# Tail of the expert stage: down 14 and its add-back ahead of gate-up 15, the last weight unit in column halves

## The reference, cut to what matters

```python
top_logit, top_idx = lax.top_k(logits, TOP_K)          # 4 of 32 experts, 256 tokens
top_w = jax.nn.softmax(top_logit, axis=-1)
gu = xb @ w_gate_up[e] + b_gate_up[e]                  # 1024 -> 2048
gate, up = jnp.split(gu, 2, axis=-1)
gate = jnp.minimum(gate, SWIGLU_LIMIT)
up = jnp.clip(up, -SWIGLU_LIMIT, SWIGLU_LIMIT)
act = (up + 1.0) * gate * jax.nn.sigmoid(SWIGLU_ALPHA * gate)
out = act @ w_down[e] + b_down[e]                      # 1024 -> 1024
y = sum over a token's 4 experts of top_w * out        # h = h + y
```

## Time and profile before

| what | us |
|---|---|
| median of 3 runs | 1254.1 |
| lowest, highest | 1253.24, 1254.36 |
| the profiled execution, its own time | 1252.16 |
| its span, first to last instruction | 1250.4 |
| TensorE busy in it | 1172.7 (94%) |
| VectorE, ScalarE busy | 302.8 (24%), 133.3 (11%) |
| transferred | 446.37 MB, mean 357 GB/s |

### The profile page before, as it was taken

The page is one execution under the profiler, slowest core; times in us unless marked ns, Lnnn a source line. Parts: engine busy times, 40 slices in busy tenths (PEclk is TensorE's granted clock), DMA queues, the critical chain, the costliest instruction groups (busy, mean ns, idle before and its releaser), DMA issues.

```text
span 1250.4 us, 14148 instructions
## 1 busy us (share of the span) xinstructions
PE 1172.7 (94%) x5825; PEld 651.9 (52%) x5825; DVE 302.8 (24%) x551; ACT 133.3 (11%) x270; POOL 6.5 (1%) x14
## 2 busy tenths in 40 slices
PE   9999999999999999989898989898898989898988
PEld 7877888888633445525353434343443424353533
DVE  2154222311302321303030303222121303030322
ACT  2233311101200010100000000001010100000001
POOL 0000001000000000000000000000000000000000
PEclk9999999999999999999999999999999999999999
DMA  9722322336799999999999999999999999999996
GB/s 379 323 99 97 119 102 101 135 135 268 279 420 427 418 428 428 428 427 428 429 428 429 430 428 428 429 429 428 428 429 428 428 429 429 428 428 430 428 420 276
DMA packets 38514, 446.37 MB, mean 357 GB/s; under 512 B 4016, under 2 KB 5168, under 8 KB 6352
## 3 DMA queue, kind: packets, MB, share of 16 engines
q1 hardware_dynamic: 37856, 443.63, 84.8%
q10 hardware_dynamic: 624, 2.25, 0.5%
HBM read 444.81 MB, written 1.05 MB: 357 GB/s over the span
## 4 chain that ended last, share of the span: by engine, by line
PE 68%; DMA 28%; issue 1%; DVE 1%; SPq 0%; ACT 0%; DVEq 0%
DMA ring<-in_w_down 21%; PE ps L512 20%; PE ps L808 16%; PE ps L831 11%; PE ps L797 4%; PE ps L771 4%; DMA arena<-in_w_down 4%; DMA ring<-in_w_gate_up 3%; PE ps L862 2%; PE ps L880 2%; PE ps L817 1%; DVE arena L1439 1%; PE ps L852 1%; PE ps L826 0%; PE ps L571 0%
## 5 line engine op out<-in xcount | busy, mean ns | idle before, releaser
L808 PE MATMUL ps<-ring,arena 128*64 128x512 f32 x1344 | 403.9, 612 | 37.3 <-DMA ring<-in_w_gate_up 32.2
L808 PEld LDWEIGHTS ps<-ring,arena 128*64 128x64 f32 x1344 | 132.6, 141 | 292.2 <-issue 292.2
L512 PE MATMUL ps<-arena,ring 128*128 128x256 f32 (+1 forms) x1184 | 268.1, 383 | 1.1 <-DVE arena L1320 1.1
L512 PEld LDWEIGHTS ps<-arena,ring 128*128 128x128 f32 x1184 | 221.0, 189 | 38.9 <-issue 6.6
L831 PE MATMUL ps<-ring,arena 128*64 128x512 f32 x672 | 200.7, 599 | 28.8 <-DMA arena<-in_w_down 19.9
L808 PE MATMUL ps<-arena 128*64 128x512 f32 x448 | 198.3, 595 | 0.0
L831 PEld LDWEIGHTS ps<-ring,arena 128*64 128x64 f32 x672 | 65.3, 138 | 148.2 <-issue 148.2
L1419 DVE COPY arena<-ps 128x1024 f32<-128x1024 f32 x16 | 19.6, 1225 | 418.8 <-PE ps L808 409.6
L831 PE MATMUL ps<-arena 128*64 128x512 f32 x224 | 101.8, 608 | 0.0
L1412 DVE TENSOR_TENSOR arena<-ps,arena 128x512 f32<-128x512 f32 x64 | 41.1, 684 | 147.4 <-PE ps L817 147.4
L1140 ACT ACTIVATE arena<-ps 128x1024 f32<-128x1024 f32 x16 | 16.4, 1024 | 557.1 <-PE ps L808 541.3
(11 more groups left out here) (210 smaller groups left out, 585.5 us busy)
## 6 DMA issues: line engine op xcount, KB each, us to landing
ring<-in_w_gate_up SPq DMA_DIRECT2D x95, 2048.0 KB, 26.9
ring<-in_w_down SPq DMA_DIRECT2D x47, 2048.0 KB, 24.2
arena<-in_w_gate_up SPq DMA_DIRECT2D x32, 2048.0 KB, 31.2
ring<-in_mix_w SPq DMA_DIRECT2D x37, 1024.0 KB, 5.4
arena<-in_w_down SPq DMA_DIRECT2D x16, 2048.0 KB, 26.1
ring<-in_w_down SPq DMA_DIRECT2D x2, 1024.0 KB, 29.0
arena<-in_consts ACTq DMA_DIRECT2D x1, 1424.0 KB, 12.4
arena<-in_xT SPq DMA_DIRECT2D x2, 544.0 KB, 4.3
```

The costliest lines, as they stand in the source:

```text
L512: last = mm(ps[:, PROJ + half, 0:rhs.shape[-1]], w[:, k, half * P:(half + 1) * P], rhs, start=(k == 0), stop=(k == KC - 1))
L808: last = mm(ps[half, bank + b], columns[:, j, half], w[x][:, at:at + 512], start=(j == 0), stop=(j == 7))
```

## The change

TensorE and SyncE get an order of their own for the end. The last 16 units are now 4 of down 14, 8 of gate-up 15 and 4 of down 15. TensorE does down 14 and add-back 14 and only then gate-up 15, hidden 15, down 15 and add-back 15. Of the gate-up units the first four are loaded as before (one expert's rows, used in twos) and the last four hold both experts' rows and are used one by one. Between the transposes of hidden 15 and down 15 stand 14 extra matmuls whose result nobody reads. The last unit of down 15 is loaded in four transfers, by column halves and experts; TensorE computes its left columns, the first group of the add-back, then its right columns and the other groups. VectorE and ScalarE follow in the same order: `weigh` and `add_up` of 14 and `weigh` of 15 ahead of `hidden` of 15, and the copy of the turned weights ahead of the sigmoid. The loop over the earlier pairs stays as it is.

```diff
--- before.py
+++ after.py
@@ -438,24 +438,31 @@
                     src = gate_up_source(lap, q) if q < 8 else down_source(lap_before, q - 8)
                     sp.dma_start(dst, src).then_inc(arrived, 16)
 
-            def last_gate_up_units(m):
+            def last_units(m):
+
+                for n in range(4):
+                    sp.wait_ge(gu_used, 8 * m + n + 5)
+                    dst, arrived, _ = place(m, n, 0)
+                    sp.dma_start(dst.rearrange("p (o n) -> p o n", o=2), down_both_source(14, n // 2, n % 2)).then_inc(arrived, 16)
                 for q in range(8):
-                    dst, arrived, _ = place(m, q, 0)
-                    slot_free(m, q)
-                    sp.dma_start(dst, gate_up_source(15, q)).then_inc(arrived, 16)
-
-            def last_down_units(m, odd, lap, first_q, pieces):
+                    sp.wait_ge(dn_used, 4 * m + q - 3)
+                    dst, arrived, _ = place(m, 4 + q, 0)
+                    if q < 4:
+                        sp.dma_start(dst, gate_up_source(15, q)).then_inc(arrived, 16)
+                    else:
+                        sp.dma_start(dst.rearrange("p (o n) -> p o n", o=2), both_experts_source(15, q)).then_inc(arrived, 16)
                 for n in range(4):
-                    dst, arrived, _ = place(m, first_q + n, odd)
-                    slot_free(m, first_q + n)
-                    src = down_both_source(lap, n // 2, n % 2)
-                    dst = dst.rearrange("p (o n) -> p o n", o=2)
-                    if n == 3 and pieces == 2:
-                        for jj in range(2):
-                            part = slice(jj * D, (jj + 1) * D)
-                            sp.dma_start(dst[:, :, part], src[:, :, part]).then_inc(tail_landed[jj], 16)
+                    sp.wait_ge(gu_used, 8 * m + 9 + n)
+                    dst, arrived, _ = place(m + 1, n, 1)
+                    if n < 3:
+                        sp.dma_start(dst.rearrange("p (o n) -> p o n", o=2), down_both_source(15, n // 2, n % 2)).then_inc(arrived, 16)
                     else:
-                        sp.dma_start(dst, src).then_inc(arrived, 16)
+                        dst = dst.rearrange("p (o j n) -> p o j n", o=2, j=2)
+                        src = w_down[30:32].rearrange("o (g p i j) n -> p g i o j n", g=2, i=2, j=2)[:, 1, 1]
+                        for c in range(2):
+                            part = slice(c * 512, (c + 1) * 512)
+                            for x in range(2):
+                                sp.dma_start(dst[:, x, :, part], src[:, x, :, part]).then_inc(tail_landed[c], 16)
 
             first_units()
             second_units()
@@ -469,9 +476,7 @@
                 lap_2 = sp.compute_val((m + 2) & 15)
                 pair_units(m, 0, lap_1, lap_0)
                 pair_units(m + 1, 1, lap_2, lap_1)
-            last_gate_up_units(last_m)
-            last_down_units(last_m, 0, 14, 8, 1)
-            last_down_units(last_m + 1, 1, 15, 0, 2)
+            last_units(last_m)
             for b in range(4):
                 sp.wait_ge(added, 4 * last_m + 5 + b)
                 sp.dma_start(out[:, 2 * b:2 * b + 2], x_sb[:, 2 * b:2 * b + 2, META:ALL]).then_inc(stored, 16)
@@ -842,9 +847,9 @@
                     if g == 1 and b == 0:
                         last.then_inc(first_half, 1)
 
-            def add_back_by_halves(m):
-
-                for b in range(4):
+            def add_back_by_halves(m, groups=range(4)):
+
+                for b in groups:
                     pe.wait_ge(eout_ready, 2 * m + 1 + b // 2)
                     pe.wait_ge(added, 4 * m - 1 + b)
                     for c in range(2):
@@ -913,7 +918,7 @@
                 for j in range(4, KC):
                     gate_up_both(j, place(0, j), xeT_1, DOWN)
 
-            def pair(m, odd=None, last_pair=False):
+            def pair(m, odd=None):
 
                 if not (isinstance(m, int) and m == 0):
 
@@ -927,26 +932,14 @@
                     pe.wait_ge(raw_copied, 4)
                 else:
                     pe.wait_ge(eout_ready, 2 * m)
-                if last_pair:
-                    down_both(landed_unit(place(m, 8, odd)), 0, 0)
-                    turn_hidden(m + 1)
-                    for n in (1, 2):
-                        down_both(landed_unit(place(m, 8 + n, odd)), n // 2, n % 2)
-                    turn_weighted(m)
-                    down_both(landed_unit(place(m, 11, odd)), 1, 1)
-                    pe.wait_ge(selwT_ready, m + 1)
-                    add_back_by_halves(m)
-                    return
-                else:
-                    down(0, [landed_unit(place(m, 8 + x, odd)) for x in range(2)])
-                    turn_hidden(m + 1)
-                    down(1, [landed_unit(place(m, 10 + x, odd)) for x in range(2)])
+                down(0, [landed_unit(place(m, 8 + x, odd)) for x in range(2)])
+                turn_hidden(m + 1)
+                down(1, [landed_unit(place(m, 10 + x, odd)) for x in range(2)])
                 turn_weighted(m)
-                if not last_pair:
-                    pe.wait_ge(sel_ready, m + 3)
-
-                    pe.wait_ge(gate_read, m + 2)
-                    gather(GATE)
+                pe.wait_ge(sel_ready, m + 3)
+
+                pe.wait_ge(gate_read, m + 2)
+                gather(GATE)
                 pe.wait_ge(selwT_ready, m + 1)
                 pe.wait_ge(eout_ready, 2 * m + 2)
                 add_back(m, isinstance(m, int) and m == 1)
@@ -969,20 +962,46 @@
             with pe.Fori(2, last_m, 2) as m:
                 pair(m, 0)
                 pair(m + 1, 1)
-            pair(last_m, 0, True)
-
+            pe.wait_ge(act_ready, last_m + 1)
+            pe.wait_ge(eout_ready, 2 * last_m)
+            for n in range(4):
+                if n == 3:
+                    turn_weighted(last_m)
+                down_both(landed_unit(place(last_m, n, 0)), n // 2, n % 2)
+            pe.wait_ge(selwT_ready, last_m + 1)
+            add_back_by_halves(last_m)
+            pe.wait_ge(xe_ready, last_m + 2)
+            pe.wait_ge(up_biased, last_m + 1)
+            for i in range(2):
+                gate_up(i, lambda q: place(last_m, 4 + q, 0), xeT)
+            for j in range(4, KC):
+                gate_up_both(j, place(last_m, 4 + j, 0), xeT)
+            turn_weighted(last_m + 1)
+            turn_hidden(last_m + 1)
+
+            pe.wait_ge(eout_ready, 2 * last_m + 2)
+            for _ in range(14):
+                mm(ps[:, DOWN + 1, 0:TOK], u2tok[:, 0, 0:P], u2tok[:, 0, 0:TOK], start=True, stop=True)
             pe.wait_ge(act_ready, last_m + 2)
-            pe.wait_ge(eout_ready, 2 * last_m + 2)
             for n in range(3):
                 down_both(landed_unit(place(last_m + 1, n, 1)), n // 2, n % 2)
-                if n == 1:
-                    turn_weighted(last_m + 1)
             w = place(last_m + 1, 3, 1)[0]
-            for jj in range(2):
-                pe.wait_ge(tail_landed[jj], 16)
-                down_both(w, 1, 1, (jj,))
+
+            def last_columns(b):
+
+                pe.wait_ge(tail_landed[b], 32)
+                for jj in range(2):
+                    for x in range(2):
+                        at = 2048 * x + 1024 * jj + 512 * b
+                        last = mm(ps[halves[x], DOWN + b], e_act[:, 6 + jj, halves[x]], w[:, at:at + 512],
+                                  start=False, stop=(jj == 1))
+                return last
+
+            last_columns(0).then_inc(first_half, 1)
             pe.wait_ge(selwT_ready, last_m + 2)
-            add_back_by_halves(last_m + 1)
+            add_back_by_halves(last_m + 1, (0,))
+            last_columns(1).then_inc(dn_used, 1)
+            add_back_by_halves(last_m + 1, (1, 2, 3))
 
 
         @block.scalar
@@ -1169,11 +1188,11 @@
                 gate_sigmoid(m + 1)
                 down_read(m)
                 weights_read(m)
-            raw_gate(last_m + 1)
-            gate_sigmoid(last_m + 1)
             weights_read(last_m)
             down_read(last_m)
+            raw_gate(last_m + 1)
             weights_read(last_m + 1)
+            gate_sigmoid(last_m + 1)
             down_read(last_m + 1)
 
 
@@ -1438,13 +1457,11 @@
                     h = x_sb[:, 2 * b:2 * b + 2, META:ALL]
                     V.tensor_tensor(h, h, add_ps[:, b % 2], ALU.add).then_inc(added, 1)
 
-            def pair(m, last_pair):
+            def pair(m):
                 weigh(m, m & 15, (m >> 4) & 3)
-                if not last_pair:
-                    select((m + 2) & 15, ((m + 2) >> 4) & 3)
+                select((m + 2) & 15, ((m + 2) >> 4) & 3)
                 hidden(m + 1, (m + 1) & 15)
-                if not last_pair:
-                    columns_read(m + 2, xeT, GATE)
+                columns_read(m + 2, xeT, GATE)
                 add_up(4 * m)
 
             select(0, 0)
@@ -1478,9 +1495,11 @@
             columns_read(2, xeT, GATE)
             add_up(0)
```

(6 more changed lines are left out.)

## The result

The changed kernel takes 1259.37 us (median of 5 runs, 1258.94 to 1261.15), the kernel before beside it 1253.24 (5 runs, 1252.30 to 1254.36): ratio 1.0052, 95% interval 1.0041 to 1.0064. It is slower, by 6.1 us where 4.9 were forecast. The predicted time itself, 1259.0, came closer than the difference did, and that is luck: I had put the difference on the median of three runs, 1254.1, which is 0.9 above the median of the runs beside the changed kernel.

A forecast was written before the change was run, and what follows sets the result against it. The prediction took TensorE, behind a full weight stream, to bound the end. Down 15 starting 4.6 us later (14.7 - 10.1) plus 0.4 for the halves gave 5.0, taken as 4.9: 1254.1 + 4.9 = 1259.0 us, range 1257.2 to 1261.5.

The forecast's parts named there:

- TensorE has the end; the stream is full: End of the kernel: TensorE sets the end, behind a transfer; weights stream at 421 to 427 GB/s, last landing 1239.1.
- Position of the last gate-up unit: Gate-up 15's last unit moves back four positions of 4.98 us, landing at 1219.2 instead of 1199.29.
- 8 KB rows: Gate-up 15's units with both experts' rows: smaller contiguous pieces could slow the stream; pace taken as 4.98 us per unit.
- Chain from gate-up 15 to down 15: Copy, transposes, DVE operations and product of hidden 15, no longer hidden: 10.1 us where 20.2 of PE work stood.
- Last unit by halves: Down 15 and add-back 15 with split last unit: 18.7 us instead of 18.3, so 0.4 later.
- Behind TensorE's end: Last add and last store: 3.7 us from PE's end to the span's, as before.
- nothing changes: The claim that after PE's end the last add and store still take 3.7 us.
- 2 KB rows: Last unit's pieces: at the stores' rate 1 MB takes 3.7 us instead of 2.5; hidden, so no cost.
- Clock: Rival: transposes count as idle, clock drops under the extra matmuls, down 15 starts 1.7 us later; 1260.7, chance 0.30.
- Landings: Rival: gate-up 15's last unit lands early and landings set the end; 1251.3, chance 0.05 faster, 0.05 same.
- Late pieces: Rival: the last unit's pieces land too late for TensorE; 1261.5 at 2.5 us over, chance 0.05.

The follow-up runs named there:

- a_again: The changed kernel run once more, unchanged: median 1259.64 us, ratio 1.0055 to the kernel before.
- a_no_extra: The changed kernel without the 14 extra matmuls under the activation of hidden 15: median 1261.44 us, ratio 1.0069 to the kernel before.
- a_single: The changed kernel with one expert's rows in all eight units of gate-up 15: median 1262.96 us, ratio 1.0081 to the kernel before.
- b_... kernels: Edits of the kernel before: column halves, both experts' rows (run twice), or two or three down 14 units ahead of gate-up 15; medians 1252.69 to 1256.41 us.
- a_rows: The changed kernel with the last unit in two pieces by rows and the add-back in one go: median 1259.21 us, ratio 1.0054 to the kernel before.
- a_turns: The changed kernel with 52 transposes in place of the 14 extra matmuls: median 1259.35 us, ratio 1.0053 to the kernel before.
- b_columns: The kernel before with the last unit by column halves, first add-back group ahead of the right columns: median 1253.30 us, ratio 1.0005 to the kernel before.

## Why the prediction was right, and where its size was off

- **TensorE has the end; the stream is full.** Right: nobody waited for the pieces, and the last one landed before TensorE came to it (1242.3; used from 1249.4). That is later than the 1239 to 1241 that I had named, since the stream as a whole was later.
- **Position of the last gate-up unit.** Right as a step (four positions). The landing at 1221.7 instead of 1219.2 is 1.3 from ahead of the changed part and 1.2 from the stream in it: one step of 1.0 that comes and goes (a_again, a_no_extra), and 0.3 for four more units with 8 KB rows (4.97 apiece instead of 4.90; with 16 KB rows in a_single the last four landed 4.89 apart), which I had named and not priced.
- **Chain from gate-up 15 to down 15.** Summed 10.1; measured 1235.38 - 1225.46 = 9.9.
- **Last unit by halves.** Summed 18.7, measured 18.9. From unit 12 on, the start of down 15 moved by 4.4 instead of 4.6, and the part behind it grew by 0.6 instead of 0.4; that their sum is met to the tenth is partly luck.
- **Behind TensorE's end.** The step "nothing changes" failed by 0.5: the slowest store took 3.0 to land, where before's took 2.5 to 2.7. All six traces of the changed order show 4.1 to 4.4 from TensorE's end to the span's; before and the six b_... kernels show 3.7. It is not the halves, which a_rows lacks. What tells the six from the seven is an instruction load: in each of the six traces a packet of 8 KB of the instruction queue, 0.6 to 0.9 us long, starts 1.4 to 1.5 us after the issue of the last store (1256.5 in the trace after) and ahead of its landing; the seven have none between the issue of their last store and its landing. That it is the cause is argued from this, since no run moved it.
- **2 KB rows.** I priced them from the stores as rows of that size. The stores' packets are of 1 KB, so the bound was looser than it said; it decided nothing.
- **Rivals.** Clock: no drop behind gate-up 15 in the traces with the extra matmuls, nor with transposes; I gave it 0.30, too much for a rule that no row supported. A drop for want of the matmuls, in a_no_extra, cost 2.7 and not the 1.7 of the earlier trace rows: it lasted twice as long. Landings: no unit came ahead of its turn; in a_no_extra the first piece of the last unit landed 1.1 ahead of the unit before it, and TensorE came to it long after. Late pieces: none.
- **Size.** 4.9 forecast, 6.1 measured; the changed kernel run again beside another set of runs of before was 7.5 above it, a_turns 5.7. 0.5 (store) and 0.3 (rows) are found. The rest of the 6.1, 0.4, is within the interval (5.1 to 8.0) and within the scatter of the stream: the loop's last unit landed at 1160.0 in the trace before and at 1160.0 to 1163.1 in the twelve others, of either order, with the same code up to there. Which part of it the place of the code in memory has, stays open.

## What to carry to other kernels

When a stream of weights sets the pace, price a reordering by what stands between a landing and the end on the engine that has the end (here TensorE), not by busy shares: a chain over several engines is nearly free only while that engine has other units to work on, and an add-back that needs VectorE and ScalarE, where it is queued behind the chain, is no such work. Splitting the last transfer wins nothing when the engine is late for it; look for its wait first. If TensorE must idle for microseconds ahead of its last work, fill the gap, and measure whether the filling has to be matmuls.

## What the runs showed of the hardware

Transposes alone, some 7.7 us of them, held TensorE's granted clock at 1.00; idling for 6.7 us brought 6.8 us at 0.50 (a_turns, a_no_extra; one trace each). A wait of 2.7 us for a landing was followed by a drop in the trace before and by none in b_columns, so that one and the same wait costs 0 or 1.8 us from one execution to the next. A load of 16 KB of instructions occupied one DMA engine for 1.1 us and went before every landing in the last 16 units that was more than 0.5 us late (7 of 7), while 19 other loads between 1181 and 1217 were followed by none as late. A load of 8 KB lay inside the last store in the six traces in which that store took 3.0 to 3.2 us, and in none of the seven in which it took 2.5 to 2.6.
